# Two weight units multiplied together with 512 moving columns, and a normalisation moved into the exponential's scale

## The reference

```python
def gmlp_branch(pc, ln_g, ln_b, w_s, b_s):          # the gating branch
    z = jax.nn.gelu(pc)
    u, v = z[..., :GMLP_D], z[..., GMLP_D:]           # v: what the kernel calls "w"
    v = layer_norm(v, ln_g, ln_b)...
    sv = jnp.einsum('gts,bnsgc->bntgc', w_s * causal, v) + b_s.T[:, :, None]
    return u * sv.reshape(b, s, GMLP_D)

def mem_cross_attention(h, mem, norm_mem_g, w_xq, w_xkv, w_xo):   # h = rms_norm(x)
    q = (h @ w_xq).reshape(b, s, XATTN_HEADS, XATTN_DH)
    kv = (rms_norm(mem, norm_mem_g) @ w_xkv).reshape(b, m, 2, XATTN_HEADS, XATTN_DH)
    k, v = kv[:, :, 0], kv[:, :, 1]
    logits = jnp.einsum('bqhd,bkhd->bhqk', q, k) * (XATTN_DH ** -0.5)
    p = jax.nn.softmax(logits, axis=-1)
    o = jnp.einsum('bhqk,bkhd->bqhd', p, v).reshape(b, s, XATTN_D)
    return o @ w_xo
```

## Time and the profile before

| | us |
|---|---|
| median of 3 runs | 1828.31 |
| range of these | 1827.86 to 1830.02 |
| profiled execution, its own time | 1827.49 |
| span of the profile (first to last instruction) | 1825.8 |

### The profile page before, as it was taken

One profiled execution on the slowest core, in us unless ns is written; L12 is line 12 of the kernel. 1 busy time (PEld: TensorE's weight loads), 2 busy tenths in 40 slices (PEclk: granted clock), 3 DMA queues, 4 the chain that ended last, 5 costly groups with the idle time before them and its releaser, 6 DMA issues. The chain is left out here.

```text
span 1825.8 us, 22422 instructions
## 1 busy us (share of the span) xinstructions
PE 1781.6 (98%) x8604; PEld 1485.8 (81%) x8604; DVE 1242.6 (68%) x1631; ACT 726.5 (40%) x942; POOL 459.8 (25%) x166
## 2 busy tenths in 40 slices
PE   9999999999999999999999999999999999999996
PEld 7889778887888788888889887788788787888885
DVE  6997656654568786577779666565744697685584
ACT  4232554433454343233423245443444444343331
POOL 3442000102013244444144400010030242444440
PEclk9999999999999999999999999999999999999998
DMA  6332122332222322232232312323232223323221
GB/s 249 123 139 93 68 86 90 110 121 93 92 93 86 123 93 93 92 107 91 103 139 93 118 69 85 110 74 134 92 108 78 92 92 116 115 73 112 93 93 47
DMA packets 28328, 186.10 MB, mean 102 GB/s; under 512 B 3480, under 2 KB 3608, under 8 KB 7740
## 3 DMA queue, kind: packets, MB, share of 16 engines
q1 hardware_dynamic: 26332, 172.64, 26.3%
q0 software_dynamic: 1648, 11.54, 1.7%
q10 hardware_dynamic: 240, 0.48, 0.1%
HBM read 179.33 MB, written 7.68 MB: 102 GB/s over the span
## 5 line engine op out<-in xcount | busy, mean ns | idle before, releaser
L1327 PE MATMUL ps<-x_hd,w_hd 128*128 128x512 f32 x1600 | 630.6, 394 | 9.2 <-DVE tmp L1031 5.3
L1328 PE MATMUL ps<-x_tl,w_hd 128*128 128x512 f32 x1600 | 626.2, 391 | 0.0
L488 POOL TENSOR_TENSOR w_tl<-raw,w_hd 128x2048 fp32r<-128x2048 f32 x78 | 361.2, 4630 | 509.2 <-ACT w_hd L577 418.7
L577 ACT ACTIVATE w_hd<-raw 128x2048 fp32r<-128x2048 f32 x155 | 297.3, 1918 | 312.5 <-PE ps L1328 259.5
L1337 PE MATMUL ps<-x_hd,w_tl 128*128 128x512 f32 x1600 | 381.2, 389 | 0.3 <-DVE w_tl L796 0.3
L1327 PEld LDWEIGHTS ps<-x_hd,w_hd 128*128 128x128 f32 x1600 | 302.3, 189 | 77.6 <-DVE tmp L1031 7.3
L1328 PEld LDWEIGHTS ps<-x_tl,w_hd 128*128 128x128 f32 x1600 | 302.3, 189 | 62.5 <-issue 0.2
L1337 PEld LDWEIGHTS ps<-x_hd,w_tl 128*128 128x128 f32 x1600 | 300.0, 188 | 62.9 <-DVE w_tl L796 0.8
L1327 PE MATMUL ps<-ring_hd,w_hd 128*128 128x512 f32 (+1 forms) x672 | 254.7, 383 | 3.8 <-DVE resid L1075 3.5
L1328 PE MATMUL ps<-ring_tl,w_hd 128*128 128x512 f32 (+1 forms) x672 | 252.3, 379 | 0.0
L796 DVE TENSOR_TENSOR w_tl<-raw,w_hd 128x2048 fp32r<-128x2048 f32 x78 | 179.0, 2295 | 106.9 <-ACT w_hd L577 70.7
(11 more groups left out here) (163 smaller groups left out, 1520.1 us busy)
## 6 DMA issues: line engine op xcount, KB each, us to landing
raw<-units SPq DMA_DIRECT2D x155, 1024.0 KB, 4.8
resid<-x_t SPq DMA_DIRECT2D x4, 512.0 KB, 8.5
bias_t<-bias_tiles POOLq DMA_DIRECT2D x8, 256.0 KB, 4.6
cg<-mem_t POOLq DMA_DIRECT2D x2, 1024.0 KB, 5.1
resid<-x_t POOLq DMA_DIRECT2D x1, 2048.0 KB, 8.9
resid_dram<-resid POOLq DMA_DIRECT2D x1, 2048.0 KB, 9.5
resid<-resid_dram POOLq DMA_DIRECT2D x1, 2048.0 KB, 9.1
out<-resid SPq DMA_DIRECT2D x4, 512.0 KB, 2.8
```

Source lines behind the costliest of these rows:

```text
L488: line.done(pool.tensor_tensor(w_tl[:, k % 2, :], raw[:, k % 2, :], w_hd[:, k % 2, :].bitcast(F32), ALU.subtract), of_unit("tail", g))
L577: line.done(act.activation(out, in_, func, **kw), *labels)
L1327: pe.matmul(dst, w_hd[:, slot, w], hd[:, src, :], start=kc == 0, stop=False)
L1328: i = pe.matmul(dst, w_hd[:, slot, w], tl[:, src, :], start=False, stop=False)
```

## The change

For `w` and `xv` the two units are multiplied together. `two_units` waits for the heads of both, moves the same 256 columns of both slots (512 in all) past each stationary tile of tokens, and then does the same with both tails. A token tile has a whole bank to itself: `w` takes banks 0 to 3 (`WIDE_PREV`: both former holders must be evacuated), `xv` banks 6 and 7. The marks `used`, `over` and `e` of both units fall together. ScalarE evacuates `w` with four instructions of 512 columns instead of eight of 256, and `xv` with one of 1024 instead of two of 512. `scores_23` stands behind the first of two token tiles, `flips_23` behind the joint unit.

The queries are evacuated without their 1/rms. VectorE writes `rsx` = 1/rms * 128^-0.5 per token, and `exps` takes it as its scale, a column of values (it was a constant); `mneg` is multiplied by it too. `spread("r1", 4)` and the copy to `r_all` go.

```diff
+WIDE_PREV = [PREV[ENTRY_OF["w", _n]] for _n in range(2)]
...
                 for qb in range(TB):
                     bank, c = X_SCORES[h][qb // 2], 4 * (h % 2) + qb
                     op(ex[:, h % 2, qb, :], ps[:, bank, MEM * (qb % 2):MEM * (qb % 2) + MEM], ACT.Exp,
-                       (f"xexp{h}",), (f"xneg{h}",) + ((f"xT{h - 2}",) if h >= 2 else ()), scale=scale,
-                       bias=mneg[:, c:c + 1], accum_out=sm[:, c:c + 1])
+                       (f"xexp{h}",), (f"xneg{h}",) + ((f"xT{h - 2}",) if h >= 2 else ()),
+                       scale=rsx[:, qb:qb + 1], bias=mneg[:, c:c + 1], accum_out=sm[:, c:c + 1])
...
-            def values(i):
-                e = ENTRY_OF["xv", i]
+            def values():
+                e = ENTRY_OF["xv", 1]
                 act.wait_ge(tensor_done, line.at(f"e{e}"))
-                op(vx[:, :, 256 * i:256 * i + 256], ps[:, 6 + i, :].rearrange("p (m e) -> p m e", m=MB),
-                   labels=(f"ev{e}",), needs=("mem_tail7",))
+                op(vx, ps[:, 6:8, :], labels=(f"ev{e}",), needs=("mem_tail7",))
...
+                            if kind == "w":
+                                if arg == 1:
+                                    for t in range(TB):
+                                        op(vn[:, t, :], ps[:, W_BANK + t, :], ACT.Gelu_apprx_tanh,
+                                           (f"ev{e - 1}", f"ev{e}"), ("n0_rs",), scale=rs0[:, t:t + 1])
+                                continue
...
                         exps(3)
-                        values(0)
                         next_head(k)
                     if k == 41:
+                        values()
                         turned(2)
                         turned(3)
-                        values(1)
...
-                                op(lambda: dve.tensor_tensor(qx[:, 2 * arg + i, :], ps[:, b + i, :], r_all, ALU.mult),
-                                   f"ev{e}", needs=(f"e{e}",), independent=i)
+                                op(lambda: dve.tensor_copy(qx[:, 2 * arg + i, :], ps[:, b + i, :]), f"ev{e}",
+                                   needs=(f"e{e}",), independent=i)
...
+            def two_units(xh, xl, tiles, unit, b, middle=None):
+
+                pe.wait_ge(scalar_done, line.at(of_unit("head", unit + 1)))
+                for t in range(tiles):
+                    if middle and t == 1:
+                        middle()
+                    for kc in range(KD):
+                        w = w_hd[:, :, 256 * kc:256 * kc + 256]
+                        a = slice(P * t, P * t + P)
+                        pe.matmul(ps[:, b + t, :], xh[:, kc, a], w, start=kc == 0, stop=False)
+                        i = pe.matmul(ps[:, b + t, :], xl[:, kc, a], w, start=False, stop=False)
+                line.done(i, of_unit("used", unit), of_unit("used", unit + 1))
+                tails_ready(unit)
+                tails_ready(unit + 1)
+                for t in range(tiles):
+                    for kc in range(KD):
+                        i = pe.matmul(ps[:, b + t, :], xh[:, kc, P * t:P * t + P], w_tl[:, :, 256 * kc:256 * kc + 256],
+                                      start=False, stop=kc == KD - 1)
+                return i
...
-                    if k == 37:
-                        spread("r1", 4)
                     if k == 41:
+                        flips_23()
                         for h in range(HEADS):
                             pv(h)
```

More of the change, by code:

```diff
@@ L178 @@
 CROSS = (39, 40, 41)
+W_BANK = 0
+WIDE_PREV = [PREV[ENTRY_OF["w", _n]] for _n in range(2)]
+assert [PAIR[ENTRY_OF["w", _n]] for _n in range(2)] == [0, 1]
+assert all(ENTRIES[ENTRY_OF[_kind, 0]][0] % 2 == 0 for _kind in ("w", "xv"))
 X_SCORES, X_TURNED, X_OUT = ((4, 5), (0, 1), (4, 5), (0, 1)), ((2, 3), (2, 3), (2, 3), (4, 5)), (0, 1, 6, 7)
@@ L344, in build @@
         ms, rs, rs0 = sb("ms", [P, 4])[:], sb("rs", [P, 4])[:], sb("rs0", [P, 4])[:]
+        rsx = sb("rsx", [P, 4])[:]
         stat, aggr = sb("stat", [P, 6])[:], sb("aggr", [P, 8])[:]
@@ L623, in exps @@
             def exps(h):
-                scale = float(P) ** -0.5
                 for qb in range(TB):
@@ L970, in cross_maxima @@
                                              AX, ALU.max), needs=(f"xqk{h}",))
-                op(lambda: dve.tensor_scalar(mneg[:, c:c + 4], mx[:, c:c + 4], -float(P) ** -0.5, None, ALU.mult),
+                op(lambda: dve.scalar_tensor_tensor(mneg[:, c:c + 4], mx[:, c:c + 4], -1.0, rsx, ALU.mult, ALU.mult),
                    f"xneg{h}", needs=(f"xexp{h - 2}",) if h >= 2 else ())
@@ L1171, in _ @@
                     if k == 37:
-                        op(lambda: dve.tensor_copy(r_all, misc), "n1_r", needs=("r1b",))
+                        op(lambda: dve.tensor_scalar(rsx, rs, float(P) ** -0.5, None, ALU.mult), "rsx", needs=("r1_rs",))
                     if k == 40:
@@ L1275, in product @@
                 b = banks(e)
-                if PREV[e] is not None:
+                if kind == "w":
+                    pass
+                elif PREV[e] is not None:
                     pe.wait_ge(evacuated_by(PREV[e]), line.at(f"ev{PREV[e]}"))
@@ L1280, in product @@
                     pe.wait_ge(evacuated_by(last), line.at((l - 1, f"ev{last}")))
-                if kind in ("w", "v"):
+                if kind == "w":
+                    for prev in WIDE_PREV:
+                        pe.wait_ge(evacuated_by(prev), line.at(f"ev{prev}"))
+                    return two_units(x_hd, x_tl, TB, unit, W_BANK)
+                if kind == "v":
                     return by_tokens(e, x_hd, x_tl, TB, unit, b)
                 if kind == "xv":
-                    return by_tokens(e, m_hd, m_tl, MB, unit, b + arg, middle)
+                    return two_units(m_hd, m_tl, MB, unit, b, middle)
                 if (kind, arg) == ("xo", 0):
@@ L1414, in pv @@
             def pv(h):
-                pe.wait_ge(scalar_done, line.at(f"xat{h}", f"ev{ENTRY_OF['xv', h // 2]}"))
+                pe.wait_ge(scalar_done, line.at(f"xat{h}", f"ev{ENTRY_OF['xv', 1]}"))
                 for m in range(MB):
@@ L1439, in conv_sums @@
                 column_sums("c", ("c_cent3",))
-            CROSS_WORK = {39: scores_01, 40: scores_23, 41: flips_23}
+            CROSS_WORK = {39: scores_01, 40: scores_23}
             for l in range(DEPTH):
@@ L1451, in _ @@
                     for e, kind, arg in UNIT_KINDS[k]:
+                        if (kind, arg) in (("w", 1), ("xv", 1)):
+                            continue
                         sums = (first_sums if k == NORM_AT[l] else (lambda: column_sums("r2")) if k == 44
-                                else CROSS_WORK[k] if k in CROSS else
+                                else CROSS_WORK[k] if k in CROSS_WORK else
                                 conv_sums if k == CLN + 2 and e == FIRST_OF[k] else None)
                         i = spatial(e, arg) if kind == "sv" else product(e, kind, arg, g, sums, KD // 2 if k == 39 else None)
-                        line.done(i, f"e{e}", *((of_unit("over", g),) if e == LAST_OF[k] else ()))
+                        both = (f"e{e + 1}", of_unit("over", g + 1)) if kind in ("w", "xv") else ()
+                        line.done(i, f"e{e}", *((of_unit("over", g),) if e == LAST_OF[k] else ()), *both)
                     if g == 0:
```

7 lines of the change are left out of this document (3 added, 4 removed).

## The result

The changed kernel takes 1832.7 us (median of 11 runs, 1831.9 to 1838.7), the kernel before beside it 1828.6 (median of 11, 1827.3 to 1831.2): ratio 1.0028, 95% interval 1.0020 to 1.0036. It is slower by a little more than the 0.2% that a measurement tells apart. The profiled execution takes 1832.7, its span 1830.9 against 1825.8.

What follows compares the result with a forecast made beforehand. TensorE, busy for 98% of the span, was taken to bound the kernel. 1827.49 + 5.5 (layer 0 wait) - 2.4 (width) - 1.8 (spread) + 0.8 (cross values) + 2.0 + 1.6 (clock) = 1833.2 us; range 1829.0 to 1836.6.

Steps and rivals of the forecast that it cites:

- The wait in layer 0: Gating pair, layer 0: TensorE waits for unit 7's head before starting unit 6; 5.5 us lost and not caught up.
- The wide matmuls: Gating pair: 512-column matmuls take 21.82 us instead of 23.03; 1.2 us saved a layer, 2.4 in all.
- Behind the pair: Units after the gating pair: later tails and ScalarE's held work fit in spare time; cost nothing.
- The spread: Between units 37 and 38: eight instructions and 0.88 us go in each layer; 1.8 us saved.
- The exponentials: Cross stage, ScalarE: a second operand column costs 0.091 us each; eight ahead of the first flip move it 0.73 us.
- The cross values: Cross stage: products wait 0.65 us for the one copy of values; stage ends 0.4 us later, 0.8 lost in both layers.
- the bound: Cross stage: if exponentials cost nothing more, the flips' end sets the products' start and a layer gains 1.0 us.
- The clock: Low clock behind TensorE's waits: 2.0 us in layer 0, 1.6 us together for the two cross-stage waits.
- The waits cost only their length: Rival, all long waits: clock kept, or lost for under 2 us in all; 1829.6, up to 1831.6 us; chance 0.22.
- The first layer catches up: Rival, layer 0: the 5.5 us vanish because VectorE would delay TensorE later anyway; 1824.1 us; chance 0.08.
- No gain from width: Rival, joint units: two runs of 256 columns stream at 0.240 us, so width saves nothing; 1836.9 us; chance 0.06.
- Lost at every long wait: Rival: low clock costs 3.0 us in layer 0 and 1.5 in each cross stage; 1835.6 us; chance 0.14.

## Why the prediction was right, and where only its total was

**The wait in layer 0** (+5.5): right, place, cause and size. 86.76 against 86.75 foretold, released by the head of unit 7; taking it away gave 6.9 us back at unit 8 and as much at unit 40. That "5.5 us stay" was argued from a wait of VectorE at 137; the ledger and this run show it.

**The wide matmuls** (-2.4): right. 21.76 us a pair for 21.82 foretold, and 1.27 us lost where the width alone was undone.

**Behind the pair** (nothing): right, the 5.7 us at unit 8 are still 5.7 where a unit of before starts at 200.02 (205.68), with no new wait between.

**The spread** (-1.8): right. From the start of unit 37 to that of unit 38 in layer 1 it is 1365.71 - 1358.97 = 6.74 us before, and 5.83 after (1368.43 - 1362.60) and with the scale alone (1365.16 - 1359.33): 0.91 a layer.

**The exponentials**: 566 ns for the 475 of before, 0.091 us more as foretold, and they move the first flip by 3.53 - 2.80 = 0.73 us between the whole change and the one without the scale.

**The cross values** (+0.4 a layer): right. With the clock kept (the cross stages filled), the products with the values start 22.09 us behind unit 40 in layer 1, 21.72 before: 0.37 later, and 0.5 by unit 42. Two small misses cancel in it: from the first flip TensorE's own rows take 14.46 us where I had 14.14, and the wait for the values is 0.32 where I had 0.65. The wide stream itself gained 0.8 where the bound said 1.0.

**The clock** (+3.6): here the parts were mis-sized, and the total came out near by luck. Without the clock the ledger is 5.5 - 2.5 - 1.8 + 1.0 = 2.2 us; the profiles differ by 5.2, which leaves 3.0. But at its places the clock cost more. At the gating pair it was 5.7 - 5.5 + 1.2 = 1.4 (predicted 2.0; over the six profiles with that wait unfilled 1.4 to 2.5). In the cross stages it was 1.7 and 2.6, measured against the filled ones, where I took "half of 1.5 each": 4.3 for 1.6.

The step that failed is the reasoning "between a wait of 1.78 that lost the clock and one of 2.60 that kept it". It took one profile for a rule. The wait of 2.60 loses the clock too, in three of the six places where I have seen it (the first profile of before, the second, and the gating pair alone, two layers each), and the waits of 3.3 and 3.5 lost it every time, so that half a stretch each was too little.

That makes 5.7 us at the places of the change, 2.7 more than are left. They come back where the change touches nothing. In layer 1 the first profile of before has 6.8 us of low clock from 1093 on; at its wait at 1139.77 it is 140.0 us behind unit 8, the changed kernel, whose stretch there is half as long, 138.5 (1143.08). Less the 0.4 that the changed kernel then loses at 1144, that is 1.1 of the 1.2 us that it gains beyond the spread between units 8 and 38. In layer 0 it gains 0.9 beyond the spread between units 8 and 40: 0.3 is the low stretch at 243, 0.3 a wait of 1.51 us at 415 that is 1.21 in the changed kernel, and the rest I can't name. Another 0.4 falls in the last 20 us. A sum that starts from one profile also takes over where the clock happened to fall in it, and I had put that at nothing.

**The rivals.** "The waits cost only their length" is out for the waits of 3.5 and 5.4 us: filling them with matmuls restored full speed at the place. "The first layer catches up" is out. "No gain from width" is out. "Lost at every long wait" (1835.6) has the mechanism nearer than my sum had: the long waits all lost it, at less than its 3.0 us in layer 0 and at more than its 1.5 in the cross stages. The Trainium skill's sentence ("TensorE: Matmul & The Clock Gate", "Why this matters for your kernels") that a gap sends the clock back agrees with the waits of 3.3 to 5.4 us in every profile; those of 2.60 went either way.

The range of 1829.0 to 1836.6 held the median, but 4 of the 11 runs lie above it, up to 1838.7, with a mean clock of 0.985 to 0.987 where the others have 0.990.

## What to carry to other kernels

Joining two units saves what the narrower matmuls cost beyond their columns (here 13 ns each, 1.3 us a pair), but moves the second unit's waits ahead by a whole unit; look first for who makes the second operand, and reorder that engine in the same change. The chain through other engines that TensorE waited for was worth more here than the matmuls around it: four reorderings on ScalarE and VectorE turned a loss of 4 us into a gain of 12. And one profile shows one outcome of the clock: judge an edit by the start of units around it, not by the total alone, and take a second profile before a clock is explained by the wait ahead of it.

## What the runs showed of the hardware that I had not expected

The same instruction stream with the same wait of 2.60 us is followed by full speed (1.00) in one execution and by half speed (0.50) in another, on a program in which this wait repeats to 0.01 us. Among the shorter waits the length does not order it: of 28 waits of 1.85 to 1.89 us ahead of a product with `ssum` (two in each of the 14 profiles) 21 were followed by a low stretch, of 28 of 1.71 to 1.73 us that VectorE's `resid` ended 6, of those of 2.60 three in six. What stands around these waits differs, and no run separates that from chance. A good part of the spread of the runs goes with the clock: the two profiled executions of the kernel before differ by 3.9 us, with 6.8 us more at low clock in the slower.

Filling a wait with matmuls whose results nobody needs kept the clock at the place (1.2 us gained behind 5.4 us of wait; 1.7 and 2.6 behind 3.5). In the cross stages the median came down by 1.3 us (2.0 against the kernel before of the session), at the gating pair the total did not follow. What decides where else the clock then falls these runs do not settle.
